# A scatter of expert gates with 256 columns a token instead of two times 128, and its way out of PSUM shared by ACT and VectorE

## The reference

```
idx = jnp.take_along_axis(cand_idx, pos, axis=-1)      # i * 128 + j of the 16 best, per token and head
gates = jax.nn.softmax(best, axis=-1)
...
u = u_tab[ii]
act = jax.nn.gelu(jnp.einsum('bthkd,btd->bthk', u, hh).astype(F32)) * gg
vv = v_tab[ii]
return jnp.einsum('bthk,bthkd->btd', act.astype(h.dtype), vv)
```

## Time and profile before

| | |
|---|---|
| median of 3 runs | 5438.2 us (5436.93 to 5446.94) |
| the profiled execution | 5458.39 us, its span 5456.6 us |
| TensorE busy | 4941.8 us, 91% |
| VectorE busy | 2604.6 us, 48% |
| ACT busy | 1654.4 us, 30% |
| mean granted TensorE clock | 0.949 |

### The profile page before, as it was taken

The page is one execution under the profiler, slowest core; times in us unless marked ns, Lnnn a source line. Parts: engine busy times, 40 slices in busy tenths (PEclk is TensorE's granted clock), DMA queues, the critical chain, the costliest instruction groups (busy, mean ns, idle before and its releaser), DMA issues. The chain is left out here.

```text
span 5456.6 us, 57168 instructions
## 1 busy us (share of the span) xinstructions
PE 4941.8 (91%) x23336; PEld 4085.9 (75%) x23336; DVE 2604.6 (48%) x4137; ACT 1654.4 (30%) x2112; POOL 204.8 (4%) x76
## 2 busy tenths in 40 slices
PE   5599688787999999999989978877799999999998
PEld 5487566576888888887868766665688888888887
DVE  5422545349844433465442254423895543244444
ACT  3223322322333332222322232222233333222222
POOL 0000200001200000000000021000020000000000
PEclk9799889888999999999989988888899999999999
DMA  4322023222445555665652212421144555565664
GB/s 178 129 93 108 25 82 124 77 81 69 145 162 187 183 174 187 199 195 164 199 196 93 111 48 69 136 83 54 55 145 156 177 180 193 171 196 190 190 199 161
DMA packets 321380, 758.99 MB, mean 139 GB/s; under 512 B 19040, under 2 KB 167264, under 8 KB 300896
## 3 DMA queue, kind: packets, MB, share of 16 engines
q1 hardware_dynamic: 321120, 755.33, 40.8%
HBM read 582.77 MB, written 168.30 MB: 138 GB/s over the span
## 5 line engine op out<-in xcount | busy, mean ns | idle before, releaser
L1672 PE MATMUL psum<-vl,ah 128*128 128x512 f32 x2048 | 800.0, 391 | 22.0 <-DVE al L1851 22.0
L1672 PE MATMUL psum<-vh,al 128*128 128x512 f32 x2048 | 799.0, 390 | 0.0
L1672 PE MATMUL psum<-vh,ah 128*128 128x512 f32 x2048 | 798.9, 390 | 0.0
L1770 DVE TENSOR_TENSOR ul<-u,uh 128x1024 fp32r<-128x1024 f32 x256 | 367.0, 1435 | 726.4 <-ACT uh L1698 724.5
L1849 DVE TENSOR_TENSOR vl<-v,vh 128x1024 fp32r<-128x1024 f32 x256 | 313.7, 1225 | 733.7 <-ACT vh L1729 733.6
L294 DVE TENSOR_TENSOR w_lo<-w,w_hi 128x1024 fp32r<-128x1024 f32 x200 | 243.8, 1225 | 767.8 <-ACT w_hi L289 767.3
L1638 PE MATMUL psum<-h_lo,uh 128*128 128x512 f32 x2048 | 518.0, 395 | 57.8 <-DVE ul L1770 57.8
L1729 ACT CAST vh<-v 128x1024 fp32r<-128x1024 f32 x256 | 268.3, 1048 | 960.2 <-PE psum L1672 921.1
L1638 PE MATMUL psum<-h_hi,ul 128*128 128x512 f32 x2048 | 508.8, 391 | 0.0
L1638 PE MATMUL psum<-h_hi,uh 128*128 128x512 f32 x2048 | 505.7, 389 | 0.0
L1638 PEld LDWEIGHTS psum<-h_lo,uh 128*128 128x128 f32 x2048 | 383.3, 190 | 135.3 <-DVE ul L1770 59.0
(11 more groups left out here) (410 smaller groups left out, 6458.7 us busy)
## 6 DMA issues: line engine op xcount, KB each, us to landing
u<-in_peer_u SPq DMA_DIRECT2D x256, 512.0 KB, 3.7
v<-in_peer_v SPq DMA_DIRECT2D x256, 512.0 KB, 3.6
gelu_of_dots<-ge SPq DMA_DIRECT2D x256, 256.0 KB, 2.1
gates_by_token<-held SPq DMA_DIRECT2D x32, 2048.0 KB, 7.6
act<-gelu_of_dots SPq DMA_DIRECT2D x64, 1024.0 KB, 6.6
gate<-gates_by_token SPq DMA_DIRECT2D x64, 1024.0 KB, 10.1
w<-in_w_fm SPq DMA_DIRECT2D x14, 2048.0 KB, 7.9
w<-in_w_gate SPq DMA_DIRECT2D x12, 2048.0 KB, 7.8
```

The lines of the kernel that those rows point to most:

```text
L1672: mm = nc.tensor.matmul(psum[:, 2 * b + half, :], w[p][:, b * P:(b + 1) * P], q[p][:, half * W:(half + 1) * W], start=(n == 0 and x == 0), ...
L1770: v.tensor_tensor(fw(ul[r]), u[r][:], fw(uh[r]).bitcast(F32), ALU.subtract).then_inc(s["u_lo"], 1)
```

## The change

Matmuls. A token's two parts are now one moving operand of 256 columns, written to 256 neighbouring words; nothing is added up in PSUM. Two tokens fill a bank, so a batch is 8 tokens (h, 64 of them a layer) in the same four banks, and there is one batch in every iteration from n = 40 to 103.

The way out. For a batch, ACT copies the high half of each token to `held` (`copy_high`), and VectorE then adds the low half from PSUM onto it (`join_gates`), which frees the banks for the next batch. Both write `held` one element every 32 words. The factor 1/4096 moves to the second half, where `low_v` becomes a three-operand instruction.

```diff
+        gate_side = lambda x: psum[:, 2:6, :].rearrange("p b (t x i) -> p x b t i", t=2, x=2)[:, x].rearrange("p b t i -> p (b t) i")
+        held8 = lambda h: held[h // 4 % 2][:, :, h % 4 * 8:h % 4 * 8 + 8].rearrange("p i t -> p t i")
...
-                    sp.wait_ge(s["gate_copied"], 2 * c + 2)
+                    sp.wait_ge(s["gate_copied"], 4 * c + 4)
...
-                def products(q):
+                def products(h):
+                    q, first = h // 2, 8 * (h % 2)
...
-                    if q:
-                        pe.wait_ge(s["gate_copied"], q)
-                    for tk in range(BT):
-                        g, t = divmod(tk, Q)
-                        bank = psum[:, 2 + tk // BANK, :].rearrange("p (i t) -> p i t", t=BANK)
-                        for x in range(2):
-                            mm = nc.tensor.matmul(bank[:, :, tk % BANK], hot_j[b][:, g, :, t], part[b][:, x, g, :, t],
-                                                  start=(x == 0), stop=(x == 1), skip_group_check=True)
+                    if h:
+                        pe.wait_ge(s["gate_copied"], h)
+                    for tk in range(8):
+                        g, t = divmod(first + tk, Q)
+                        bank = psum[:, 2 + tk // 2, :].rearrange("p (t x i) -> p t x i", t=2, x=2)
+                        mm = nc.tensor.matmul(bank[:, tk % 2], hot_j[b][:, g, :, t], part[b][:, :, g, :, t],
+                                              start=True, stop=True, skip_group_check=True)
...
-                    q, r = divmod(n - HOT0 - 3, 2)
-                    if 0 <= q < NBT and r == 0:
-                        products(q)
-                pe.wait_ge(s["gate_copied"], NBT)
+                    if 0 <= n - HOT0 - 2 < 2 * NBT:
+                        products(n - HOT0 - 2)
+                pe.wait_ge(s["gate_copied"], 2 * NBT)
...
-                def copy_gates(q):
+                def copy_high(h):
...
-                    a.activation(held[c % 2][:, :, k * BT:(k + 1) * BT].rearrange("p i (g t) -> p g i t", t=BANK),
-                                 psum[:, 2:2 + BT // BANK, :].rearrange("p g (i t) -> p g i t", t=BANK), ACT.Copy, scale=1.0 / GSCALE).then_inc(s["gate_copied"], 1)
+                    a.copy(held8(h), gate_side(0)).then_inc(s["high_copied"], 1)
...
-                    q, r = divmod(n - HOT0 - 4, 2)
-                    if 0 <= q < NBT and r == 0:
-                        copy_gates(q)
+                    if 0 <= n - HOT0 - 3 < 2 * NBT:
+                        copy_high(n - HOT0 - 3)
...
-                        v.wait_ge(s["gate_mm"], q - 1)
+                        v.wait_ge(s["gate_mm"], 2 * q - 2)
...
+                def join_gates(h):
+                    v.wait_ge(s["high_copied"], h + 1)
+                    v.tensor_tensor(held8(h), gate_side(1), held8(h), ALU.add).then_inc(s["gate_copied"], 1)
...
-                    v.tensor_tensor(x, x, gate[g % 2][:, :, r, :], ALU.mult).then_inc(s["gated"], 1)
+                    v.scalar_tensor_tensor(x, gate[g % 2][:, :, r, :], 1.0 / GSCALE, x, ALU.mult, ALU.mult).then_inc(s["gated"], 1)
...
+                    if 0 <= n - HOT0 - 3 < 2 * NBT:
+                        join_gates(n - HOT0 - 3)
```

More of the change, by code:

```diff
@@ L1483, in experts_stage @@
 def experts_stage(nc, m, io, l, h_hi, h_lo, val, idx, u, below, gates_dram, dots_dram, psum):
-    BT, Q, BANK = 16, 2, 4
+    BT, Q = 16, 2
     G = BT // Q
@@ L1496, in experts_stage @@
                                    "iota_in", "dve_step", "sums_ready", "marked", "numbered", "added_up", "best_in", "exp_done",
-                                   "listed", "turned", "list_copied", "gate_lo", "ids_made", "hot_i", "hot_j", "weighed", "gate_mm", "gate_copied",
+                                   "listed", "turned", "list_copied", "gate_lo", "ids_made", "hot_i", "hot_j", "weighed", "gate_mm", "high_copied", "gate_copied",
                                    "gate_out0", "gate_out1", "v_in0", "v_in1", "g_in0", "g_in1", "d_in0", "d_in1", "v_hi", "v_lo", "gated",
@@ L1714, in copy_lists @@
                     a.mul(lists[:, 2, ts], bank[:, 2 * P:3 * P], GSCALE).then_inc(s["list_copied"], 1)
-                def copy_gates(q):
-                    c, k = divmod(q, HT // BT)
-                    a.wait_ge(s["gate_mm"], q + 1)
+                def copy_high(h):
+                    c, k = divmod(h, HT // 8)
+                    a.wait_ge(s["gate_mm"], h + 1)
                     if k == 0 and c >= 2:
                         a.wait_ge(gate_out[c % 2], 16 * (c // 2))
-                    a.activation(held[c % 2][:, :, k * BT:(k + 1) * BT].rearrange("p i (g t) -> p g i t", t=BANK),
-                                 psum[:, 2:2 + BT // BANK, :].rearrange("p g (i t) -> p g i t", t=BANK), ACT.Copy, scale=1.0 / GSCALE).then_inc(s["gate_copied"], 1)
+                    a.copy(held8(h), gate_side(0)).then_inc(s["high_copied"], 1)
                 def high_v(n):
```

## The result

| | before | after |
|---|---|---|
| median, us | 5438.1 (5436.9 to 5448.4, 6 runs) | 5473.0 (5458.2 to 5474.1, 6 runs) |
| span of the profiled execution, us | 5456.6 | 5472.3 |
| mean granted clock | 0.949 | 0.942 |

The ratio of the runs is 1.0052 [1.0037, 1.0066]: slower by about 28 us (20 to 36), where 38 us less were forecast. (The medians lie 35 us apart; the executions of both kernels scatter over 11 to 16 us, and the ratio takes all of them.) The time lies outside the range and on the other side of zero.

The account below looks back on a forecast made before the run. TensorE was taken to bound the kernel. A scatter gain of 87 us less 50 us of stalls gave -37 us from 5438, written as 5400 us; the range was 5355 to 5428 us.

Parts of the forecast that it names:

- The bound: Expert stage: TensorE sets the pace; every nanosecond off its scatter shows, as long as nobody makes it wait.
- The scatter's gain: Scatter matmuls on TensorE: 228 us become 141 at 0.120 us a matmul, a gain of 87 us.
- The lower bound: Scatter matmuls of 256 columns: fastest pace considered, 0.107 us each, a gain of 100 us.
- The add: VectorE's add onto held, per batch of 8 tokens: 2.2 us, between 1.23 and some 2.1 to 2.2.
- The copy: ACT's copy from PSUM to held, per batch: 1.04 us, at most 1.88.
- rival 2: Way out by ACT and VectorE: both copy and add slow, stalls 71 us, sum -16, 5422 us; 15%.
- The stall's mechanism: Behind each gates' store, late u delays cast, copy, add, then TensorE: 30 stalls of 1.66 us, 50 us.
- rival 3: Scatter matmuls in all 128 batches no faster per column: -15 us at 0.16, +16 at 0.213; 12%.
- rival 1: VectorE's add fast (1.23 us), late u costs 21 us: 5372 us, or 5359 with pace 0.107; 30%.
- Clock: stalls of 2 us leave it there, no term: TensorE's granted clock in the expert stage stays at 1.00 despite stalls of 2 us; nothing added.
- The rest: Second half's three-operand gating (15 us of VectorE, hidden), one-hots, the store's wait for adds: nothing added.
- The slower side: Scatter matmuls at 0.213 us, with short stalls: +16 us, 5454 us; chance of slower 0.05.

Follow-up runs that it names:

- e1: The changed kernel with the store of gates issued behind the load of the next tile of u; 5345.3 us, ratio 0.9813 to the kernel before.
- e4: The changed kernel with ACT's copy ahead of its cast and VectorE's add ahead of the low part; 5335.6 us, ratio 0.9807 to the kernel before.
- e6: The kernel before, its 128-column scatter matmuls kept but written to neighbouring PSUM words, ACT reading PSUM in steps; 5338.8 us, ratio 0.9812.
- e7: The changed kernel with its 256-column matmuls writing every fourth PSUM word (gates in its output wrong); 5471.2 us in one run, against 5446.2 before.
- e9: The changed kernel with ACT's copy alone running over the 8 tokens innermost; 5409.7 us, ratio 0.9945 to the kernel before.
- e3: The changed kernel with both copy and add running over the 8 tokens innermost; 5390.8 us, ratio 0.9894 to the kernel before.

## Why the prediction was wrong

The time is outside the range on the slow side for two reasons: one cost was taken at half its size (point 4), and one cost was put at nothing (point 6).

1. **The bound** was read rightly: what TensorE saves in this stage shows, as long as nobody makes it wait (e1, e4, e6: 102 to 105 us saved, all of it in the end).
2. **The scatter's gain**: the right direction, under-sized, 105 for 87 us. The term taken was 0.120 a matmul, from an f32r row, and 0.14 for the change back; measured 0.104 and 0.13. The lower bound (0.107, 100 us) was the nearer one. The prediction left open whether the step or the number of matmuls was the cause, since both gave the same sum; e6 and e7 show that it is the step.
3. **The add** (2.2 us): right, 2.23 to 2.27. It was taken from a row that steps in its read alone, and in f16; that a stepped write beside it adds nothing was an assumption, and it came true.
4. **The copy** (1.04 us): this step failed. It was argued from the earlier trace rows that ACT steps 128 bytes without loss; but the old instruction did so after each run of four neighbouring words, and a run of one wasn't in the trace. Measured 2.06, beyond even the upper bound of 1.88. That bound was half the pace, 1.66 ns an element and the constant part (1.88 - 2048 x 0.83 ns = 0.18 us); measured are (2.06 - 0.18) / 1024 = 1.84 ns, so the step costs more than a doubling. That both ways out are slow was rival 2, given 15%.
5. **The stall's mechanism** was right in every link: only behind the store of gates, 30 times, cast, copy, add, TensorE. **Its size** was wrong, a wait of 2.97 us for 1.66 (TensorE goes on 3.13 us late). In the cycle shown, which is longer than the mean: cast at g + 10.76 for 10.09 (+0.67), copy 1.97 for 1.04 (+0.93), wanted at g + 12.6 for 12.9 (+0.3); together 1.9, less 0.1 for a faster add. Over all 30, e9, which has the copy as forecast, is 2.11 us late: the copy is 1.0 of the 1.5 us that were missing, the later `u` and the earlier wanted time the rest. The latter was foreseeable: a faster batch brings the wanted time forward, so what raises the gain raises the stall as well. The forecast worked that out for a slower matmul (rival 3), not for a faster one (the 0.107 in rival 1). The ratio of e9 is 0.9945 where the forecast's was 5400/5438 = 0.993. That is near in part by luck: 18 us more of gain stand against 13 more of stalls and 9 of clock.
6. **"Clock: stalls of 2 us leave it there, no term"**: this was the second failed step, and it decides the sign. Its ground was a mean of 1.00 over a stretch in which TensorE never waited, and that says nothing of stalls. Waits of 2.97 us did not leave it at 1.00, and cost some 39 us more; without that the sum would be -105 + 94 = -11. For the stalls it spoke of the sentence is nearly right (5 of the 20 stalls between 1.9 and 2.4 us in all profiles have slow matmuls behind them, none of the 88 shorter ones), but a forecast with 2.4 us stalls in it (rival 2) needed the term, and had no price for it. Rival 2 came to -87 + 71 = -16; measured are -105 + 94 + 39 = +28.
7. **The rest** held. The three-operand gating costs 686 ns for 687; the row of 748 ns in the earlier trace rows misled, and it was hidden anyway. The one-hots delay TensorE by 2.6 us in all. The second half is no longer.
8. **The slower side** was placed in the matmul (rival 3, priced +16). e7 shows what that would have been: no gain and shorter stalls. The slower side that came was the stall, and no rival carried a stall larger than the gain.

What stays open: why the issue of the store takes 1.1 to 1.5 us in 8 of 16 cases of the first layer after (about 1.0 to 1.25 in 4 of 16 of the second) and mostly 0.43 in the others; why `u` is late by a few tenths even where it doesn't; and what decides whether the clock falls. In all profiles 27 of the 31 stalls above 2.6 us have slow matmuls behind them, 7 of the 11 between 2.4 and 2.6, and 5 of the 108 below that; nothing was run that separates the length of the stall from what came before it.

## What to carry to other kernels

A stage that gets shorter exposes the transfers it used to hide: for each of them compute when it lands and when it will be wanted after the change, with the gain itself in the wanted time, and list what is queued in order behind the instruction that waits for it; here moving one issue, or swapping two instructions, was worth 130 us. Give an engine's idling its price in clock wherever a stall term reaches some microseconds at full clock. When the order of elements has to be turned on the way out of PSUM, let TensorE write neighbouring words, let the engine that takes them out read PSUM in long steps, and let it write runs of neighbouring words to SBUF.

## What the runs showed of the hardware

- TensorE's output in steps of four PSUM words nearly halves its pace: 0.107 against 0.057 us for 128 f16 columns, 0.194 against 0.104 for 256. The weight load in front of such a matmul reads 97 ns at neighbouring words (after, e6) and 135 with the step (before, e7).
- Reading PSUM in steps of 256 words costs ACT and VectorE nothing that shows (e3: 1.02 and 1.22 us for 1024 elements, where a cast from SBUF takes ACT 1.05 and the low part VectorE 1.22).
- ACT writing single f32 words 128 bytes apart in SBUF: 2.06 to 2.10 us for 1024 elements, against 1.02 in runs of eight. Runs of four are as fast as runs of 16 (1.88 and 1.89 us for 2048). VectorE reading and writing single words so: 2.23 to 2.29 against 1.22.
- Granted clock 0.60 over the 4.3 us behind a stall of 3.2 us, at 1.00 before and after: 1.57 us lost. It fell behind 27 of 31 stalls above 2.6 us, 12 of 31 between 1.9 and 2.6, and none of 88 shorter ones.
